# Expert biases by ScalarE instead of TensorE in a two-block transformer kernel, with a rearranged first expert block, split first tiles, and the second norm inside the last loop turn

## What is computed

```python
def expert_block(args):
    xb, e = args
    gu = xb @ w_gate_up[e] + b_gate_up[e]
    gate, up = jnp.split(gu, 2, axis=-1)
    gate = jnp.minimum(gate, SWIGLU_LIMIT)
    up = jnp.clip(up, -SWIGLU_LIMIT, SWIGLU_LIMIT)
    act = (up + 1.0) * gate * jax.nn.sigmoid(SWIGLU_ALPHA * gate)
    return act @ w_down[e] + b_down[e]
```

## Time and profile before

| what | value |
|---|---|
| median of 3 runs | 2074.31 us (2073.28 to 2075.12) |
| the profiled execution's own time | 2073.48 us |
| its span in the profile | 2071.6 us |
| PE busy | 2040.2 us, 98% |
| PEld, DVE, ACT, POOL busy | 79%, 75%, 55%, 12% |
| granted PE clock | full in nearly all of the span |
| HBM traffic | 251 GB/s over the span |
| expert loop | about 249 to 1379 us of the span |

### The profile page before, as it was taken

One profiled execution on the slowest core, in us unless ns is written; L12 is line 12 of the kernel. 1 busy time (PEld: TensorE's weight loads), 2 busy tenths in 40 slices (PEclk: granted clock), 3 DMA queues, 4 the chain that ended last, 5 costly groups with the idle time before them and its releaser, 6 DMA issues.

```text
span 2071.6 us, 26310 instructions
## 1 busy us (share of the span) xinstructions
PE 2040.2 (98%) x9284; PEld 1628.6 (79%) x9284; DVE 1555.5 (75%) x1435; ACT 1136.9 (55%) x1055; POOL 240.5 (12%) x249
## 2 busy tenths in 40 slices
PE   8999999999999999999999999989999999999998
PEld 5865478888888888888888888858888878888887
DVE  6987499999999999999999999985674443333333
ACT  3132277777777777777777777754114632222222
POOL 0006311111111111111121211110000000000000
PEclk9999999999999999999999999999999999999999
DMA  5233599999999999999999999941132213222321
GB/s 227 92 142 120 211 392 399 389 387 376 385 381 385 379 384 377 387 376 385 379 383 381 377 385 377 386 177 61 67 96 83 82 41 112 102 100 83 122 82 41
DMA packets 79158, 522.71 MB, mean 252 GB/s; under 512 B 10352, under 2 KB 10880, under 8 KB 22144
## 3 DMA queue, kind: packets, MB, share of 16 engines
q1 hardware_dynamic: 66496, 483.88, 59.8%
q0 software_dynamic: 9056, 30.62, 5.8%
q10 hardware_dynamic: 3552, 7.46, 1.1%
HBM read 501.31 MB, written 18.60 MB: 251 GB/s over the span
## 4 chain that ended last, share of the span: by engine, by line
PE 94%; DVE 3%; DMA 1%; issue 1%; ACT 1%; SPq 0%; DVEq 0%; ACTq 0%
PE bank L1116 26%; PE bank L1118 26%; PE bank L1117 26%; PE bank L1108 4%; PE bank L1125 1%; PE bank L1314 1%; PE bank L1463 1%; DMA ring<-in_wmoe 1%; PE bank L1265 1%; PE bank L1306 1%; PE bank L1154 1%; PE bank L1542 1%; PE bank L1523 1%; PE bank L1558 1%; PE bank L1505 0%
## 5 line engine op out<-in xcount | busy, mean ns | idle before, releaser
L1884 DVE TENSOR_TENSOR ring_r<-ring,room_r 128x2048 fp32r<-128x2048 f32 x384 | 875.3, 2294 | 76.4 <-ACT room_r L770 70.2
L770 ACT ACTIVATE room_r<-ring 128x2048 fp32r<-128x2048 f32 x384 | 736.1, 1918 | 175.5 <-PE bank L1118 165.1
L1117 PE MATMUL bank<-ring_r,room_r 128*128 128x512 f32 x1744 | 678.8, 389 | 0.0
L1116 PE MATMUL bank<-room_r 128*128 128x512 f32 x1576 | 622.9, 395 | 4.1 <-DVE ring_r L1884 3.9
L1118 PE MATMUL bank<-room_r 128*128 128x512 f32 x1568 | 611.4, 390 | 0.0
L1117 PEld LDWEIGHTS bank<-ring_r,room_r 128*128 128x128 f32 x1744 | 327.8, 188 | 69.0 <-issue 3.1
L1116 PEld LDWEIGHTS bank<-room_r 128*128 128x128 f32 x1576 | 295.9, 188 | 66.4 <-DVE ring_r L1884 5.9
L1118 PEld LDWEIGHTS bank<-room_r 128*128 128x128 f32 x1568 | 294.3, 188 | 62.7
L1116 PE MATMUL bank<-room_r,ring_r 128*128 128x512 f32 x520 | 203.5, 391 | 1.8 <-DVE ring_r L2046 0.9
L1118 PE MATMUL bank<-room_r,ring_r 128*128 128x512 f32 x512 | 199.3, 389 | 0.0
L1117 PE MATMUL bank<-ring_r 128*128 128x512 f32 x384 | 149.5, 389 | 0.0
(11 more groups left out here) (297 smaller groups left out, 2159.4 us busy)
## 6 DMA issues: line engine op xcount, KB each, us to landing
ring<-in_wmoe SPq DMA_DIRECT2D x384, 1024.0 KB, 12.7
ring<-in_wf SPq DMA_DIRECT2D x33, 1024.0 KB, 4.8
ring<-in_wd SPq DMA_DIRECT2D x7, 2048.0 KB, 9.3
ring<-in_wp SPq DMA_DIRECT2D x14, 1024.0 KB, 4.8
ring<-in_wo SPq DMA_DIRECT2D x2, 2048.0 KB, 9.3
ring<-in_wd SPq DMA_DIRECT2D x2, 1024.0 KB, 8.7
room<-in_xtok ACTq DMA_DIRECT2D x1, 2048.0 KB, 12.6
h_rows<-room POOLq DMA_DIRECT2D x4, 512.0 KB, 3.0
```

The source lines that it names most:

```text
L770: act.activation(w_hi[s_ % PAIRS], raw_w[ORDER[s_]], ACT.Copy)\
L1116: pe.matmul(out, x_hi, w_hi, start=start, stop=False, skip_group_check=True)
L1117: pe.matmul(out, x_hi, w_lo, start=False, stop=False, skip_group_check=True)
L1884: dve.tensor_tensor(w_lo[i], raw_w[i], w_hi[s_ % PAIRS].bitcast(F32), ALU.subtract)\
```

## The change

- **Biases.** `biases`, `select`, `sel_all`, `sel_cur` and the split bias table are gone. SP loads the expert's bias row (8 KB) into one partition ahead of each block's pieces; POOL spreads it over all partitions with one `partition_broadcast` of 2048 columns (`spread_bias`), from where `select` stood; ACT writes it into banks 0 to 3 (`seeds`, two instructions of 128x512 per pair of banks) and PE's first product adds to what is there. The "+1" for the up half, once done by POOL, is ACT's bias operand.
- **Banks and order.** The gathered rows are transposed into banks 4 and 5 instead of 0 and 1, so `turn(b, 1)` moves behind the next block's wait for `x_lo`, and PE waits for `act_lo` ahead of `gathered` instead of behind it.
- **First block.** `ple_proj` and the last two `bias_down` come ahead of the last `ple_gate`. Steps 0, 1 and 4 are split ahead of the block, in a different set of buffers (`pair`), and PE waits for the first seed.
- **First tiles.** Tiles 2 and 3 of the mixer input use split products, so ACT and DVE split one more piece each.
- **Second norm.** ACT's and DVE's code for it moves, unchanged but for the order of `half_lo(0)`, into the branch of the last loop turn.

Core of the diff (semaphore counts that only shift by one are left out):

```diff
             def block_loads(b, first):
                 expert = sp.value_load(meta[0:1, bass.ts(b, 1)], min_val=0, max_val=E - 1)
+                if not first:
+                    sp.wait_ge(s["bias_spread"], b)
+                sp.dma_start(bias_row, a["bgu"][bass.ts(expert, 1), :]).then_inc(s["bias_in"], 16)
...
-            def select(b):
-
-                pool.tensor_copy(sel_cur, sel_all[:, bass.ds(b, 1)].broadcast_to([P, P])).then_inc(s["sel_ready"], 1)
+            def spread_bias(b, first):
+
+                wait_counted("bias_in", b * 16 + 16)
+                if not first:
+                    wait_counted("seeded", b * CHUNKS)
+                pool.partition_broadcast(bias_wide, bias_row).then_inc(s["bias_spread"], 1)
...
             def block_pool(b, first):
 
                 wait_counted("rows_in", b * 16 + 16)
+                if not first:
+                    spread_bias(b, first)
                 wait_counted("xt_ready", b + 1)
...
                 keep_rows(b)
 
-                wait_counted("used", after(b, PLACE[4]))
-                select(b + 1)
...
+            chunk(act, 0)
+            act.activation(w0_hi, w0_raw, ACT.Copy).then_inc(s["zhi_done"], 1)
             z_hi(1)
...
                 if g == 2 * TT - 2:
 
                     split_hi(0, 0, True)
+                    split_hi(0, 1, True)
+                    split_hi(0, 4, True)
...
+            def seeds(b, c, first=False):
+
+                if c == 0:
+                    act.wait_ge(s["bias_spread"], b + 1)
+                    if first:
+                        act.wait_ge(s["bdn_done"], 2 * TT)
+                    else:
+                        act.wait_ge(s["x_lo"], b + 1)
+                elif not first:
+                    act.wait_ge(s["act_ready"], b * CHUNKS)
+                for h in range(2):
+                    q = 2 * c + h
+                    ins = act.activation(bank[q][:, :], bias_wide[:, q * 512:(q + 1) * 512], ACT.Identity if h else ACT.Copy,
+                                         **(dict(bias=ones[:, 0:1]) if h else {}))
...
                 sigmoids(b - 1, 1)
                 gathered_hi(b)
                 split_hi(b, 1)
+                seeds(b, 0)
                 split_hi(b, 2)
                 turned_hi(b - 1, 1)
-                for s_ in range(3, 8):
+                split_hi(b, 3)
+                seeds(b, 1)
+                for s_ in range(4, 8):
                     split_hi(b, s_)
...
                     with act.If(T < b + ROUNDS):
                         rest_act(T)
+                        second_block_rows()
...
             def block_pe(b, first):
                 pe.wait_ge(s["x_lo"], b + 1)
-                pe.wait_ge(s["sel_ready"], b + 1)
-                biases(0)
+                if not first:
+                    turn(b - 1, 1)
+                if first:
+                    pe.wait_ge(s["pool_steps"], 4)
+                pe.wait_ge(s["seeded"], b * CHUNKS + 1)
                 gate_up(b, 0, first)
...
-                biases(1)
+                pe.wait_ge(s["seeded"], b * CHUNKS + 2)
                 gate_up(b, 6)
                 gate_up(b, 7)
                 turn(b, 0)
                 gate_up(b, 8)
                 gate_up(b, 9)
+                pe.wait_ge(s["act_lo"], b * CHUNKS + 1)
                 gathered(b + 1)
                 if not first:
                     pe.wait_ge(s["y_copied"], b * 2)
-                pe.wait_ge(s["act_lo"], b * CHUNKS + 1)
                 down(b, 10)
                 down(b, 11)
-                turn(b, 1)
```

More of the change, by code:

```diff
@@ L401, in landed, with pair @@
             eng.wait_ge(raw_in[i], b * 16 if i >= 10 else b * 16 + 16)
+        def pair(first, s):
+            return {1: 2, 4: 3, 5: 1}.get(s, s % PAIRS) if first else s % PAIRS
         def counted(edge, s):
@@ L430, in xt_bank @@
         def xt_bank(b, q):
-            return bank[6 + q] if isinstance(b, int) and b == 0 else bank[q]
+            return bank[6 + q] if isinstance(b, int) and b == 0 else bank[4 + q]
         def ffn_used(f):
@@ L840, in first_chunk @@
                 split_hi(b, 11, first)
-            split_hi(0, 1, True)
-            for s_ in range(4, 9):
+            seeds(0, 0, True)
+            split_hi(0, 5, True)
+            seeds(0, 1, True)
+            for s_ in range(6, 9):
                 split_hi(0, s_, True)
@@ L1133, in _ @@
                 first_tile(j, range(2, KT)).then_inc(s["z_ready"], 1)
-            chunk(pe, 0)
+            pe.wait_ge(s["zlo_done"], 3)
             for j in range(2, 4):
-                first_tile(j, range(KT)).then_inc(s["z_ready"], 1)
+                at = (j % 2) * P
+                for k in range(KT):
+                    ins = product(bank[j][:, :], w0_hi[:, k, at:at + P], w0_lo[:, k, at:at + P], x_hi[:, k, :], x_lo[:, k, :],
+                                  k == 0, k == KT - 1)
+                ins.then_inc(s["z_ready"], 1)
             def z_tile(j):
                 c = j // 4
-                pe.wait_ge(s["zlo_done"], 2 + c)
+                pe.wait_ge(s["zlo_done"], 3 + c)
                 pe.wait_ge(s["z_evac"], j - 3)
@@ L1308, in turn @@
                 ins.then_inc(s["turned"], 1)
-            def biases(c):
-                for h in range(2):
-                    q = 2 * c + h
-                    pe.matmul(bank[q][:, :], sel_cur, bias_tab[:, q * 512:(q + 1) * 512], start=True, stop=False,
-                              skip_group_check=True)
             def gate_up(b, s_, first=False):
@@ L1944, in first_chunk @@
                 activations(b, 0)
-                split_lo(b, 9, first)
-                split_lo(b, 10, first)
+                split_lo(b, 9, first, first)
+                split_lo(b, 10, first, first)
                 turned_lo(b, 0)
-                split_lo(b, 11, first)
-            split_lo(0, 1, True)
-            for s_ in range(4, 9):
-                split_lo(0, s_, True)
+                split_lo(b, 11, first, first)
+            for s_ in range(5, 9):
+                split_lo(0, s_, True, True)
             first_chunk(0, True)
@@ L2036, in _, with rest_dve @@
-            second_norm(1)
-            combine(2)
-            first_root(1).then_inc(s["x2_ready"], 1)
-            combine(3)
-            second_norm(2)
-            second_norm(3)
-            first_rms(2)
-            first_rms(3)
-            for k in range(KT):
-                dve.wait_ge(s["uT_done_a"], k + 1)
-                dve.scalar_tensor_tensor(uT_lo[k], bank[k][:, :], pcol("norm1", k), uT_hi[:, k, :].bitcast(F32),
-                                         ALU.mult, ALU.subtract).then_inc(s["uT_done_v"], 1)
+            def rest_dve(b):
+                activations(last, 1)
+                split_lo(b, 2, True)
+                turned_lo(last, 1)
+                split_lo(b, 3)
@@ L2050, in _, with more_dve @@
+            def more_dve(b):
+                with dve.If(b[0] < T):
+                    block_dve(b[0])
+                    if b[1:]:
+                        more_dve(b[1:])
+            with dve.Fori(1, BLOCKS + 1, ROUNDS) as b:
+                with dve.If(b <= T):
+                    more_dve([b + q for q in range(ROUNDS)])
+                    with dve.If(T < b + ROUNDS):
+                        rest_dve(T)
+                        second_block_rows()
             half_lo(2)
```

194 lines of the change are left out of this document (97 added, 97 removed).

## The result

| | us |
|---|---|
| before, median | 2074.65 (2073.28 to 2075.12) |
| changed, median | 2096.95 (2095.86 to 2098.22) |
| ratio, 95% interval | 1.0109 (1.0097 to 1.0122) |
| forecast, with its range | 2065.0 (2040 to 2105) |

The change makes the kernel 22 us slower, where the forecast was 9 us faster. The time is inside the range and close to the 2097 that the prediction gave for a broadcast of 3 us, but that is luck: the broadcast takes 2.30 us, and most of the loss lies elsewhere.

The account below looks back on a forecast made before the run. PE was taken as the bound, busy 98% of the span. Biases -10.2, first block +3.3, first tiles -1.5, second norm -0.9, table loads +1.0 sum to -8.3, rounded -8.5: from 2073.5 to 2065.0 us, range 2040 to 2105.

Parts of the forecast that it names:

- Biases on PE, 31.3 us: Expert loop: dropping two bias matmul pairs spares PE 1.01 us a block, 31.3 us over 31 blocks.
- The hold, X - 1.3: Block border: POOL's broadcast, taking X (1.98 us), holds DVE for X - 1.3, a stall of 0.68 us a block.
- The slack: Block border: room between DVE's x_lo, ACT's seeds and PE's products, taken as nothing, between that and 0.46 us.
- +1, between 0 and +9: Loop: two table loads of 1.28 us in each of 11 turns, 28 us of ACT, cost +1 us.
- the lost race: Block border: broadcast gets in ahead of the second split_lo, so all of it delays DVE: +30 + 1.7, 2105 us.
- +3.3, between -2 and +5: First block: the last gate, held by two bias_down, ends later, partly offset by removed waits: +3.3 us.
- the four terms: First block, gate's end to PE's start: rows' high part 0.87, low part 1.0, biased sum 1.28, seeds 1.3 us.
- -0.9, between -3 and +1: Behind the loop: with last turn and sums reordered, DVE's first norm instruction comes some 0.9 us earlier: -0.9 us.
- First tiles, -1.5: Mixer input tiles 2 and 3: split products save PE 2.9 us, convolution paced by ACT and DVE: -1.5 us.
- The stream of weights: Rival, loop: weight DMA becomes the bound; kept at 381 GB/s no gain, 2075 us; chance 0.09, with a balance near nothing.
- The rival of a slower broadcast: Border: broadcast slower than a copy, losing from X = 2.3; 2097 at 3 us, 2149 at 4.7; chance 0.33.
- in order of issue: POOL and DVE instructions with two inputs in SBUF exclude each other, the one issued first going first.

Follow-up runs that it names:

- half a broadcast: Changed kernel with the second norm back behind the loop, and only 1024 of 2048 bias columns broadcast in the loop: 2057.22 us, ratio 0.9914.
- the norm put back: Changed kernel with the second norm of ACT and DVE back behind the loop: 2079.02 us, ratio to before 1.0022.
- the early seeds: Changed kernel with the broadcast in the block's first third and the first pair of seeds written half a block earlier: 2061.85 us, ratio 0.9942.
- two broadcasts in a row: Changed kernel with the second norm back behind the loop, and the broadcast done twice, one behind the other: 2266.12 us, ratio 1.0924.
- the early seeds for block 0: Changed kernel with block 0's first pair of seeds written after 6 of the 8 biased sums instead of all 8: 2087.55 us, ratio 1.0064.

## Why the prediction was wrong

- **Biases on PE, 31.3 us: right in kind.** 0.90 us a block measured, 27.9 us.
- **The hold, X - 1.3: right.** The place, the three instructions, the cover of 1.3 us and the order of events are as predicted, and half a broadcast shows the cover by itself. X was 1.98 by the copies; 2.30 was measured, 2.0 of it exclusive, and L1971 is held for 0.93 us, not 0.68. The 1.00 us for 1024 columns are well under the 1.8 cycles a column that the Trainium skill gives as the best case for a tight loop (GPSIMD Engine Reference, section 3.1), which would have made it an estimate of 1.5 us for 1024. The slack was taken as 0 and is 0.4. These two errors offset each other, so it is in part luck that a border costs 34.82 - 34.17 = 0.65 us against the 0.68 forecast. The gain is 0.25 a block against 0.33.
- **"+1, between 0 and +9" for the table loads: this step failed.** It counted what a load costs ACT ("only the first of a pair stands ahead of something urgent, by at most 0.8 us"). It did not ask what the load does to the race between POOL and DVE, though the prediction itself priced the lost race at about 1 us a block and set it aside for all borders because of the branch. At a third of the borders the load decides it, and not the branch: 12.9 us, and 3 for the clock behind the longer waits. With the loads gone, 15.9 us.
- **"+3.3, between -2 and +5" for the first block: failed, +13.3.** The later gate was right in mechanism, and its wait measured 3.1 us. The chain from the gate's end to PE's start was right too, 6.1 us predicted and 6.2 measured, though the four terms that it names add up to 4.45: the two `gated` instructions (1.4 us) are not among them. What failed is that the clock was taken as full behind these waits. Half clock costs 1.4 us in the gate (PE starts at 260.07, not 258.6; with the norm put back the gate ran at full clock, and PE starts at 259.02), 2.9 at the block's start (the product forecast for 266.8 comes at 271.17) and 1.6 behind its first `turn`. Besides, the broadcast for block 1 made PE wait 2.3 us in block 0, where only the loop's borders had been looked at, and the 1 us of further waits that the early splits should remove wasn't there. The prediction called the product at 261.88 step 1's; it is step 5's, and step 1's, at 254.47, had a wait of 2.19 us of its own.
- **"-0.9, between -3 and +1" for the second norm and the last sums: failed, +5.2.** The table's -1.6 is the four moved matmuls, and nothing is gained ahead of the second block. That the norm starts earlier is worth 1.6 us (the row is 33.7, and 35.3 with the norm put back), but only against the new order of the last sums with the norm behind the loop; the two cancel. What was left out is that work which stood behind a branch, with time to spare, now has the branch right behind it: a table load and a late start of DVE's next instruction, 5.1 us in the 216 products.
- **First tiles, -1.5: -0.4,** within the range, and as said given back.
- **The stream of weights is no bound** at a period of 34.17: with the early seeds PE is busy in all of 350 us, at 385 GB/s.

Together: -9.1 for the biases in the loop (31 periods of the kernel with the norm put back, less the 1.7 us of moved matmuls), +15.9 for the loads, +13.3, +5.2 and -0.4 make the 24.8 us, with -0.1 elsewhere.

The rival of a slower broadcast had the right sign and by chance the right time, for a broadcast that takes 3 us. The term for the table loads was not a price read badly from a row: it left out one of those whom the load delays.

## What to carry to other kernels

Price an instruction that is added to an engine not by its own time but by who gets ahead of whom after it, in each of the kernel's places that differ (first block, first block of a loop turn, last). DVE was busy 94% of the loop here, and a delay of it in the first third of a block still reached the border; to move the work that waits for it off the border gave 31 us, to move the delay some 4 us. And look for waits that can be shorter than written: the early seeds for block 0 were one changed number and a moved call, worth 9 us.

## What was not expected of the hardware

- A POOL copy of 96x1 took 4.34 us beside two `split_lo` that followed each other without a pause (4.48 us for both), and got in between them at none of the ordinary borders. Where DVE had a pause it took 1.8 us, and in the kernel before, where the two took 4.83, it took 2.24. But in block 0 of the changed kernel a broadcast did get in between two `split_lo`, though ACT's part for the second was there in time and DVE made no pause. So what lets POOL in stays open.
- Of two broadcasts in a row the second took 5.50 us, since DVE stayed ahead of it. The Trainium skill says that the order of issue decides who blocks, and, of a DVE instruction in a 2-port mode, that whoever issues first holds the shared ports for its whole instruction (SBUF — State Buffer, section "Who interferes with whom"). The borders of the changed kernel agree with that, with 1.62 us on DVE at an ordinary one and 3.85 at a loop turn's start; this second broadcast, issued first by its record and last to finish, does not. In the earlier trace rows it is so too: DVE's L1820 begins at 182.66, ahead of POOL's L557 at 182.83, and still ends with it. So "in order of issue", as the prediction has it, is right at the borders and no more than that.
- A PE wait of 1.5 us in two parts was followed by half clock at two of ten like borders, costing as much as the waits themselves.
